# A two-layer DiT block: modulation halves divided between scan and gating, x read back in mixing

## What is computed

```python
for layer in range(DEPTH):                                  # DEPTH = 2
    mod = (c_s @ ada_w[layer] + ada_b[layer])[:, None, :]
    sh1, sc1, g1, sh2, sc2, g2 = jnp.split(mod, N_MOD, axis=-1)
    ...
    hl = rmsnorm(x, norm_mix_w[layer]) * (1.0 + sc1) + sh1
    y_l, y_c = mixer(hc, hl, ...)     # retention, window attention, gated delta net, @ w_out
    x = x + g1 * y_l
    x = x + g2 * swiglu(rmsnorm(x, norm_ffn_w[layer]) * (1.0 + sc2) + sh2, ...)
return rmsnorm(x, final_norm_w)
```

## Time and profile before

| | us |
|---|---|
| median of 3 runs | 4062.64 (4061.82 to 4066.37) |
| the profiled execution's own time | 4066.5 |
| its span, first to last instruction | 4064.7 |
| TensorE busy over the span | 3520.0 (87%) |
| VectorE, ScalarE, GpSimd busy | 1589.4, 1073.4, 646.9 |
| mean granted clock of TensorE | 0.924 |

### The profile page before, as it was taken

One profiled execution on the slowest core, in us unless ns is written; L12 is line 12 of the kernel. 1 busy time (PEld: TensorE's weight loads), 2 busy tenths in 40 slices (PEclk: granted clock), 3 DMA queues, 4 the chain that ended last, 5 costly groups with the idle time before them and its releaser, 6 DMA issues. The chain is left out here.

```text
span 4064.7 us, 54588 instructions
## 1 busy us (share of the span) xinstructions
PE 3520.0 (87%) x20668; PEld 2942.1 (72%) x20668; DVE 1589.4 (39%) x2595; ACT 1073.4 (26%) x1927; POOL 646.9 (16%) x758
## 2 busy tenths in 40 slices
PE   5989666968697999999998989667866879999998
PEld 3778565846585888888885878556755758888886
DVE  3466634632324222222236465634621342222324
ACT  2343123621204121211213343123511131221112
POOL 1134633221100000000001234532222000000000
PEclk8999887988698999999999999888987889999999
DMA  4455374069201111111111465373096111111111
GB/s 161 138 182 187 91 206 130 27 181 303 99 21 37 36 41 36 36 41 36 40 37 71 151 197 164 107 205 110 18 274 198 42 36 47 49 49 46 46 52 57
DMA packets 281909, 405.19 MB, mean 100 GB/s; under 512 B 108675, under 2 KB 184707, under 8 KB 280966
## 3 DMA queue, kind: packets, MB, share of 16 engines
q1 hardware_dynamic: 277894, 392.39, 31.1%
q0 software_dynamic: 3840, 10.49, 0.7%
HBM read 292.08 MB, written 110.70 MB: 99 GB/s over the span
## 5 line engine op out<-in xcount | busy, mean ns | idle before, releaser
L901 PE MATMUL ffn_bank<-ffn_h_hi,ffn_w_hi 128*128 128x512 f32 (+1 forms) x1760 | 650.7, 370 | 18.1 <-DVE ffn_h_lo L314 18.1
L904 PE MATMUL ffn_bank<-ffn_h_lo,ffn_w_hi 128*128 128x512 f32 (+1 forms) x1760 | 650.0, 369 | 0.0
L905 PE MATMUL ffn_bank<-ffn_h_hi,ffn_w_lo 128*128 128x512 f32 (+1 forms) x1760 | 649.4, 369 | 0.0
L811 PE MATMUL frt_acc<-frt_w_hi,frt_h_hi 128*128 128x472 f32 x960 | 374.8, 390 | 48.5 <-DVE frt_w_lo L688 27.5
L901 PEld LDWEIGHTS ffn_bank<-ffn_h_hi,ffn_w_hi 128*128 128x128 f32 x1760 | 333.3, 189 | 75.8 <-DVE ffn_h_lo L314 18.1
L904 PEld LDWEIGHTS ffn_bank<-ffn_h_lo,ffn_w_hi 128*128 128x128 f32 x1760 | 333.2, 189 | 55.4
L905 PEld LDWEIGHTS ffn_bank<-ffn_h_hi,ffn_w_lo 128*128 128x128 f32 x1760 | 333.0, 189 | 55.7
L811 PE MATMUL frt_acc<-frt_w_hi,frt_h_lo 128*128 128x472 f32 x960 | 368.1, 383 | 0.0
L811 PE MATMUL frt_acc<-frt_w_lo,frt_h_hi 128*128 128x472 f32 x960 | 365.3, 381 | 0.0
L895 DVE TENSOR_TENSOR ffn_w_lo<-ffn_raw,ffn_w_hi 128x1024 fp32r<-128x1024 f32 x132 | 161.8, 1226 | 502.0 <-ACT ffn_w_hi L891 496.8
L901 PE MATMUL ffn_bank<-ffn_a_hi,ffn_w_hi 128*128 128x512 f32 (+1 forms) x880 | 324.3, 369 | 0.8 <-DVE ffn_a_lo L969 0.8
(11 more groups left out here) (310 smaller groups left out, 5699.5 us busy)
## 6 DMA issues: line engine op xcount, KB each, us to landing
ffn_raw<-w_ffn SPq DMA_DIRECT2D x132, 512.0 KB, 3.2
x<-ada_w SPq DMA_DIRECT2D x20, 2048.0 KB, 10.9
proj<-frt_out SPq DMA_DIRECT2D x120, 236.0 KB, 2.0
x<-proj SPq DMA_DIRECT2D x60, 384.0 KB, 4.5
frt_raw<-w_in SPq DMA_DIRECT2D x96, 236.0 KB, 4.5
pack<-frt_side SPq DMA_DIRECT2D x80, 256.0 KB, 2.5
scn_fd<-feat SPq DMA_DIRECT2D x40, 384.0 KB, 8.2
met_pr<-proj SPq DMA_DIRECT2D x20, 704.0 KB, 5.5
```

What stands on the lines that cost most here:

```text
L811: mm = pe.matmul(acc[q % NA][:, 0:GW], a[:, k, tok], b[:, k, :], start=(k == 0 and i == 0), stop=(k == KC - 1 and i == 2))
L901: mm = pe.matmul(out, w_hi, b_hi, start=first, stop=False)
L904: pe.matmul(out, w_hi, b_lo, start=False, stop=False)
L905: return pe.matmul(out, w_lo, b_hi, start=False, stop=last)
```

## The change

The pieces of the modulation are divided. Beside the scan run vectors 2 to 4 of layer 0 (six halves) and 2 to 3 of layer 1 (four). Beside the gating run vector 5 of layer 0 with the first two of layer 1 (six halves), and vectors 4 and 5 of layer 1 (four). Gating loads all gate columns at once, into the room of `yr_lo`, without waiting for a buffer, and its loop carries the halves. x is no longer read in gating but in mixing, in eight transfers that GpSimd issues when the first two weights have landed, and VectorE waits for a block's transfer before it adds to it. VectorE's loop in mixing is written out.

```diff
-def mix_part(layer):
-    return layer, 0, 2
-
-
-def rest_part(layer):
-    return layer, 2, NMOD - 2
+def beside_scan(layer):
+    return [(layer, 2, 3)] if layer + 1 < DEPTH else [(layer, 2, 2)]
+
+
+def beside_gate(layer):
+    return [(layer, 5, 1), (layer + 1, 0, 2)] if layer + 1 < DEPTH else [(layer, 4, 2)]
...
 def gated(...)
-        gin = [st.sb(f"gin{u}", [P, 2, 256]) for u in range(4)]
+        gin = yr_lo[:].bitcast(F32).rearrange("p a n -> p (a n)").rearrange("p (k b n) -> p k b n", k=10, b=2)
...
+        def halves(k):
+
+            return [i for i in range(m.halves) if (i + 1) * NU // m.halves - 1 == k]
...
                 for k, (g, i) in enumerate(UNITS):
-                    if k >= 4:
-                        sp.wait_ge(s["turned"], k - 3)
                     row = row_of(t0 + 2 * g)
-                    sp.dma_start(gin[k % 4][:], proj[...]).then_inc(ins[k % 4], 16)
+                    sp.dma_start(gin[:, k], proj[...]).then_inc(ins[k], 16)
                     if k == 3:
-                        sp.dma_start(nw[:], norm_w[layer]).then_inc(s["set_in"], 16)
-                        sp.dma_start(x[:], x_copy).then_inc(s["x_in"], 16)
-
-                sp.wait_ge(s["x_in"], 16)
+                        m.sync_load(sp, 0)
+                sp.dma_start(nw[:], norm_w[layer]).then_inc(s["set_in"], 16)
+                m.sync_small(sp)
+                for i in range(1, m.halves):
+                    m.sync_load(sp, i)
...
                     spread(k)
+                    for i in halves(k):
+                        m.tensor_product(pe, i)
+                        if i:
+                            m.tensor_turn(pe, i - 1)
+                m.tensor_turn(pe, m.halves - 1)
...
+                m.scalar_begin(act)
                 act.preload_act_table(ACT.Sqrt)
...
                     round_(k)
+                    for i in halves(k):
+                        m.scalar_copy(act, i)
+                m.scalar_end(act)
...
 def mixed(...)
+            @block.gpsimd
+            def _(pool):
+                for u in range(2):
+                    pool.wait_ge(w.landed[u], 16)
+                    pool.sem_inc(weights_first, 1)
+                for m in range(KC):
+                    pool.dma_start(x[:, m, lo:TOK], x_copy[:, m, lo:TOK]).then_inc(x_in[m], 16)
...
-                def add(n, u):
+                def add(m):
+                    n, u = divmod(m, 2)
+                    dve.wait_ge(x_in[m], 16)
```

More of the change, by code:

```diff
@@ L115, in __init__ @@
         self.bias, self.product = alloc("m_bias", [NM]), alloc("m_product", [NM, 2])
-        self.nw = alloc("m_nw", [len(parts), KC])
+        self.scales = [(i, turn) for i, (layer, first, n) in enumerate(parts) for turn in (1, 4) if first <= turn < first + n]
+        self.smalls = 16 * (1 + len(parts) + len(self.scales))
+        self.nw = alloc("m_nw", [max(len(self.scales), 1), KC])
         self.acc, self.cols = st.ps("m_acc", [P, 512]), st.ps("m_cols", [P, 512])
@@ L135, in sync_small @@
             sp.dma_start(self.bias[:, at:at + n * KC], self.ada_b[layer][:, first * KC:(first + n) * KC]).then_inc(self.small_in, 16)
-            sp.dma_start(self.nw[:, i, :], self.norms[0 if first == 0 else 1][layer]).then_inc(self.small_in, 16)
             at += n * KC
+        for j, (i, turn) in enumerate(self.scales):
+            sp.dma_start(self.nw[:, j, :], self.norms[0 if turn == 1 else 1][self.parts[i][0]]).then_inc(self.small_in, 16)
     def sync_load(self, sp, i):
@@ L200, in gpsimd_end @@
                                self.bias[:, here].unsqueeze(2).broadcast_to([P, n * KC, 2]), ALU.add).then_inc(self.mod_done, 1)
[L201 to L206, removed]
+        pool.wait_ge(self.mod_done, len(self.parts))
+        for j, (i, turn) in enumerate(self.scales):
+            mod, amix, affn = self.mods[self.parts[i][0]]
+            out = amix if turn == 1 else affn
+            pool.tensor_scalar(out[:], mod[:, turn * KC:(turn + 1) * KC, :], 1.0, None, ALU.add).then_inc(self.plus_one, 1)
+            pool.wait_ge(self.plus_one, j + 1)
+            pool.tensor_tensor(out[:], out[:], self.nw[:, j, :].unsqueeze(2).broadcast_to([P, KC, 2]), ALU.mult).then_inc(self.scale_done, 1)
+        pool.wait_ge(self.scale_done, len(self.scales))
 def modulation(nc, parts, cs, ada_w, ada_b, norms, ident, mods):
@@ L2140, in _, with mixed @@
                 rest(NU - 1)
-def mixed(nc, layer, lo, x, units, mod, ys, yr):
+def mixed(nc, layer, lo, x, x_copy, units, mod, ys, yr):
     chunk = lambda half, k: ys[half][:, k - 2] if 2 <= k < 6 else yr[half][:, k % 6 + (2 if k >= 6 else 0)]
```

47 lines of the change are left out of this document (24 added, 23 removed).

## The result

| | before | after |
|---|---|---|
| median, us | 4064.51 (4061.82 to 4067.62, 4 runs) | 4019.66 (4013.35 to 4021.49, 4 runs) |
| the profiled execution's own time | 4066.5 | 4013.35 |
| its span | 4064.7 | 4011.6 |

The ratio is 0.9887, 95% interval 0.987 to 0.9904. The medians differ by 44.9 us; the forecast was 41. The profiled execution of after lies 6.3 us under its median and that of before 2.0 above, so differences of stages add up to more than 45.

What follows compares the result with a forecast made beforehand. The scan was taken to wait for transfers, gating's loop and mixing to be bound by TensorE. Terms -45 - 15 + 23 - 4 = -41 us gave a median of 4022 us, range 3999 to 4050.

Steps and rivals of the forecast that it cites:

- The scan, -45: Both scans: fewer weight loads in the queue, and fewer small steps, save 45 us, from 30 to 59.
- the slope between the layers: Scan: 16.6 us between the layers' eight tiles for four more loads, so 4.15 us per load.
- the sign by which it was to be judged: Scan: the prediction is wrong if waits for `scn_rk` stay as long with half the loads.
- The front of gating, -15: Start of gating: the stall becomes one 2 MB weight load, not 5 MB of x; saves 15 us, from 10 to 18.
- The loop, +23: Gating's loops: the added halves cost 14 and 9 us, with the clock going up and down.
- between 0 and +55: Gating's loops: cost 0 if the products bring the full clock, 55 us if all stays at half clock.
- the first rival: Gating's loops: the clock rises for the whole loop, which then costs nothing; 3999 us, chance 0.14.
- The tail, -4: End of gating: the last half covers VectorE's last steps, leaving a copy and GpSimd's modulation; saves 4 us.
- Mixing, 0: Mixing: reading x there costs nothing, as its blocks land in time or their lateness is covered.
- The sign given for it: Mixing: VectorE's first addition would be released by TensorE and not by a transfer.
- the cover: Mixing: the additions have 11 us before the weights they hold up are wanted, so late x costs nothing within that.
- the slower rival: Mixing: x arrives late, deciding below 47 GB/s; at 35 GB/s it loses 72 us, giving 4094 us, chance 0.04.

Runs made afterwards that it cites:

- all_in_scan: The changed kernel with all halves beside the scans and none in gating, its new loading kept: 4036.87 us, ratio 0.9926.
- idle_short: all_in_scan plus three matmuls of 512 columns, result unread, behind every spread in gating: 4054.79 us, ratio 0.9983.
- idle_products: all_in_scan plus 16 matmuls of 512 columns, result unread, at each of the changed kernel's product places in gating's loop: 4148.22 us, ratio 1.0205.
- product_first: The changed kernel with each product in gating's loop ahead of the spread instead of behind it: 4044.29 us, ratio 0.9951.
- copy_first: The changed kernel with ScalarE copying gating's last half before it rounds the last unit: 4011.19 us, ratio 0.9873.
- weights_last: The changed kernel with gating's first weight load behind all gate columns and small inputs, not behind the fourth block: 4007.99 us, ratio 0.9862.
- x_early: The changed kernel with x's eight loads issued at the start of mixing, without waiting for the first two weights: 4020.55 us, ratio 0.9897.
- x_late: The changed kernel with x's loads issued only when the first block of mixing's products is done: 4021.93 us, ratio 0.9896.

## Why the forecast was right, point by point

**The scan, -45.** Measured -43.7 in the two profiled executions. Over more of them it is less: with the scan of before (before, all_in_scan, idle_short, idle_products) the stages average 191.0 and 168.2 us, with that of after (after, product_first, copy_first, weights_last, x_early, x_late) 165.1 and 154.5, which makes -39.6, 4.0 us for each half, where the slope between the layers had said 4.15. Its least promised part, that a last tile takes about 10 us, came too: 1002.0 - 992.15 = 9.8. From the second tile to the last it was 113.8 and 103.5 us, where 111 and 102 stood. That the loads carry most of it is shown by the kernel without them, where TensorE's busy time fell by 17.8 of the 46.5 us with a higher granted clock, a way of gaining that the forecast did not have. Not right was the sign by which it was to be judged: the waits for `scn_rk` did not fall in proportion. PE's waits in the scan of layer 0, before and after:

```profile
PE scn_b_z L1622 <- DMA scn_rk<-feat: 57.2, 8, 22.1
...
PE scn_b_z L1627 <- DMA scn_rk<-feat: 46.6, 7, 21.4
```

Of the 46.6 us 21.4 are the first tile's own arrival and 10.0 the two loads behind it, both as before; the other five make 15.2, where the other six made 24.8. In layer 1 the sum fell from 49.2 to 45.1. So only 14.7 of the 43.7 us are such waits; over both scans TensorE's busy time fell by 29.7 us (134.9 to 117.8 and 122.4 to 109.8), mostly the product and turning of the halves that left.

**The front of gating, -15.** Measured -7.4 and -8.6. What was left of the stall was one weight load, as the forecast had it: weights_last takes off 5.1 and 5.4 us more.

**The loop, +23.** This term was mis-sized. From the first sums to the end of the last turning it is 1068.16 - 1024.60 = 43.6 us and 34.8 us, before 36.8 and 29.4: +12.2. The choice "between 0 and +55" took a clock going up and down near 0.7, which was too low: it was 0.80 to 0.87 and 0.72 to 0.78 in the six executions with this order of the loop, nearer to the first rival than to the middle, and with it the loop costs about half of the 23 us. It did go up and down, but stayed up for most of the time. That it came up at all behind spread and product, as the earlier trace rows had suggested, is right, and product_first shows that their order matters. The Trainium skill ("TensorE: Matmul & The Clock Gate", section on the HAM clock gate) says that sustained activity releases the slow clock. Taken by itself, that is not what this loop shows: all_in_scan has 36 us without idle time at 0.50, and with matmuls of 512 columns in the same loop the clock was 0.90 to 0.96.

**The tail, -4.** From TensorE's last instruction to mixing's first, 8.1 and 7.9 us before are 6.2 and 5.9 after, -3.9 in sum. What was not seen is the wait of 1.47 us per layer ahead of the last turning, the copy behind the rounding; it is part of the loop's 12.2.

**Mixing, 0.** Measured -0.3 and +1.1. The sign given for it was wrong, since the first addition was released by the transfer; it was the cover that made this harmless, and x_late shows it. The forecast gave the additions 11 us; in x_late the first was 15.8 us late and nothing was lost. The eight blocks, 5.24 MB, landed within 19.5 us of the first one's issue, some 270 GB/s, and only the first was waited for in layer 0: the slower rival, below 47 GB/s, did not come.

The terms as measured, -43.7 - 16.0 + 12.2 - 3.9 + 0.8, are -50.6 us of the 53.1 between the two profiled executions; 2.5 are in stages that were not touched. The forecast's sum came close partly by cancelling: the scan gives some 5 less over many executions, and the loop costs 11 less. That these two errors nearly cancel is luck; that each stage moved the way forecast is not.

## What to carry to other kernels

Where weights for later share a queue with transfers that are wanted now, price the load from two stages that run the same work with different numbers of loads, and then look at the first load of all: it stands behind the fewest bytes and in front of the first consumer, and moving it by a few lines gave 11 us in gating here. Work moved into a stretch at half clock may raise the clock of all that stands there, as the products of 512 columns did here (0.50 to 0.87 and 0.78); the same products at another place did less (0.67 and 0.61), so try the place. Before crediting a division of work with a gain, run it undivided with everything else changed; here the division had some 17 of 45 us.

## What was not expected of the hardware

In gating's loop TensorE was busy without a gap at a granted clock of 0.50 for 36 us; three matmuls of 512 columns behind each spread made it 0.90, and the same product ahead of the spread or behind it 0.67 or 0.87. The 16 records of a modulation product, in four quarters of the array, took 1.90 us; 32 records of the same width in one place took 13.89 us at the full clock, 0.43 each against 0.12; that the place makes the difference was not tried by itself. With ten weight loads left out of a scan, the same 1368 records of matmuls kept TensorE busy for 125.5 us and not 135.7, at a granted clock of 0.94 and not 0.85. Issuing a tile's 15 transfers takes SP's queue 9 us by itself (844.71 to 853.96 in layer 0, some 0.6 each), a large share of a tile's pace of 13 us. And a transfer of 640 KB took 12.1 us in the median to land when eight were issued together with weights, without costing the stage anything.
